# Rewriting the expert stage of a one-core decoder layer: a ring of slots for each of two gathered tables, and the weighted sum shared by TensorE and VectorE

## The reference, cut to what matters

```
a   = gelu(einsum('td,thkd->thk', h, u[e]))        # 128 dot products of 1024 for each token
out = einsum('thk,thkd->td', gate * a, v[e])       # 128 weighted rows summed
x   = x + g2 * out;  y = rms_norm(x, final_g)
```

## Time and profile before

| | us |
|---|---|
| median of 3 runs | 6320.8 |
| span of the profiled execution, first to last instruction | 6308.8 |
| what lies around the span (median less span) | 12.0 |
| expert stage, first instruction to the end of the span (3239.70 to 6308.8) | 3069.1 |
| POOL busy in the whole span | 2370.1 |
| DVE busy in the whole span | 2487.9 |
| PE busy in the whole span | 4576.8 |

### The profile page before, as it was taken

How to read it: one execution, slowest core, us unless ns; L and a number is a source line. 1 busy time by engine, 2 the same in 40 slices (tenths; PEclk the granted TensorE clock), 3 DMA queues, 4 the chain that set the end, 5 groups by cost and what they waited for, 6 DMA issues and landing times. The chain is left out here.

```text
span 6308.8 us, 40559 instructions
## 1 busy us (share of the span) xinstructions
PE 4576.8 (73%) x11996; PEld 2161.0 (34%) x12036; DVE 2487.9 (39%) x5373; ACT 897.6 (14%) x1904; POOL 2370.1 (38%) x2136
## 2 busy tenths in 40 slices
PE   6999999976777767877746657656666566566666
PEld 2444444434444443433212222222222222222222
DVE  2000000004443344799974443443544444444434
ACT  1000000012222210111101011111111111111111
POOL 0000000000000000000037777777777777777776
PEclk8999999987767777988868878878878888788788
DMA  6144434641010033111049999999999999999998
GB/s 238 49 143 142 139 121 142 211 177 50 28 45 37 33 137 147 54 43 39 9 154 338 357 361 366 366 351 368 365 359 369 354 368 366 352 369 356 363 365 302
DMA packets 395337, 1409.24 MB, mean 223 GB/s; under 512 B 39803, under 2 KB 91683, under 8 KB 390500
## 3 DMA queue, kind: packets, MB, share of 16 engines
q0 software_dynamic: 297504, 1083.18, 45.8%
q1 hardware_dynamic: 72118, 272.53, 12.3%
q10 hardware_dynamic: 25664, 52.88, 2.2%
HBM read 1341.66 MB, written 159.08 MB: 238 GB/s over the span
## 5 line engine op out<-in xcount | busy, mean ns | idle before, releaser
L1577 PE MATMUL ex_acc<-ex_V,ex_diag 128*128 128x512 f32 x4096 | 1916.5, 631 | 960.3 <-ACT ex_diag L1601 882.1
L1663 DVE CUSTOM_DVE_ANT_0 ex_U<-ex_U,ex_h 128x1024 f32<-128x1024 f32 x1024 | 1195.5, 1223 | 1560.5 <-DMA ex_U<-in_peer_u,ex_idx 1438.7
L1577 PEld LDWEIGHTS ex_acc<-ex_V,ex_diag 128*128 128x128 f32 x4096 | 827.8, 204 | 2047.1 <-issue 1094.3
L1534 POOL DMA_INDIRECT ex_U<-in_peer_u,ex_idx x1024 | 1178.4, 1151 | 362.3 <-issue 334.8
L1534 POOL DMA_INDIRECT ex_V<-in_peer_v,ex_idx x1024 | 1150.6, 1124 | 312.1 <-issue 308.1
L390 PE MATMUL z_ps<-win,hT 128*128 128x464 f32 x3024 | 1188.0, 554 | 14.6 <-ACT z_stage L372 9.5
L390 PEld LDWEIGHTS z_ps<-win,hT 128*128 128x128 f32 x3024 | 538.9, 179 | 663.0 <-issue 648.5
L1518 POOL DMA_INDIRECT ex_U<-in_peer_u,ex_idxT x8 | 7.6, 949 | 1868.0 <-DVE ex_idxT L1631 1865.9
L466 POOL DMA_DIRECT2D mx_masks<-table_masks x1 | 0.7, 706 | 1362.3 <-POOLq L139 1362.3
L720 DVE TENSOR_SCALAR mx_xb<-mx_O,mx_ab 128x128 f32<-128x128 f32 x32 | 9.0, 344 | 1233.1 <-PE mx_O L533 1233.1
L1596 ACT ACTIVATE ex_u<-ex_u 128x16 f32<-128x16 f32 x64 | 13.8, 216 | 2478.6 <-DVE ex_u L1442 2082.7
(11 more groups left out here) (333 smaller groups left out, 3429.2 us busy)
## 6 DMA issues: line engine op xcount, KB each, us to landing
out_kv_w_sample<-in_cache_kv_w SPq DMA_DIRECT2D x8, 8188.0 KB, 41.6
win<-in_w_in SPq DMA_DIRECT2D x21, 1856.0 KB, 10.1
z_scratch<-z_stage ACTq DMA_DIRECT2D x21, 1856.0 KB
ada<-in_ada_w SPq DMA_DIRECT2D x12, 2048.0 KB, 7.8
ex_U<-in_peer_u,ex_idx POOLq DMA_INDIRECT x1024
ex_V<-in_peer_v,ex_idx POOLq DMA_INDIRECT x1024
out_kv_w_sample<-in_cache_kv_w SPq DMA_DIRECT2D x8, 2044.0 KB, 17.1
mx_zg<-z_scratch SPq DMA_DIRECT2D x8, 1544.0 KB, 7.2
```

What stands on the lines that cost most here:

```text
L1534: pool.indirect_dma_start(out=buf[n][:, :], out_offset=None, in_=table, in_offset=bass.IndirectOffsetOnAxis(ap=idx[b][:, n:n + 1], axis=0) ...
L1577: last = nc.tensor.matmul(acc[:, b, :], dg[:, n, :], V[n][:, b * 512:(b + 1) * 512], start=False, stop=False)
L1663: nc.vector.tensor_tensor_reduce(out=U[n][:, :], in0=U[n][:, :], in1=h2[:, :], scale=1.0, scalar=0.0, op0=ALU.mult, op1=ALU.add, accum_out ...
```

## The change

All slots are numbered through, 0 to 1023 for the prompt and 1024 to 1031 for the samples, and every engine's program is written out slot by slot, without loops.

- U and V have rings of 12 buffers each; slot n uses buffer n % 12. POOL issues 4 gathers of U, then 4 of V, and so on. Each gather waits for the use of the slot 12 earlier. The indices are read where routing left them, without a copy.
- DVE waits for each U slot by itself, makes its dot, and after every 4 slots the gelu for these 4: now through Tanh, in four small operations with the Tanh on ACT between the third and the last.
- The weighted sum is shared. Odd slots go to PE as before, with 4 diagonal buffers. Even slots are summed on DVE: `acc = V * w + acc`, a `scalar_tensor_tensor` on 128 x 1024 with V and acc in SBUF (for the first slot of a tile `tensor_scalar` without acc).
- The tail adds acc to PE's sum first, one operation more. The store moves from ACT's queue to SP's. There are two h2 buffers.
- The samples come last, after the prompt's gathers; their gathers, too, wait for slots of the ring.

```diff
 def experts(k, misc):
+GRP, RING, DIAGS = 4, 12, 4
+def on_pe(slot): return slot >= PROMPT_SLOTS or slot % 2 == 1
...
             @block.gpsimd
-                pool.wait_ge(s["idxT"], 1)
-                for n in range(NS):
-                    pool.indirect_dma_start(out=U[HALF + n][:, :], ...)
-                    pool.indirect_dma_start(out=V[HALF + n][:, :], ...)
-                def head(i, pair, b):
-                    nc.gpsimd.tensor_copy(idx[b][:, :], k.idx[:, bass.ds(i * P + h * NSLOT, NSLOT)])
...
+                def gather_u(slot, index):
+                    if slot >= RING:
+                        pool.wait_ge(s["dots"], slot - RING + 1)
+                    pool.indirect_dma_start(out=half(slot), out_offset=None, in_=u_dram,
+                                            in_offset=bass.IndirectOffsetOnAxis(ap=index, axis=0)).then_inc(loaded[slot % RING], 16)
+                def gather_v(slot, index):
+                    if slot >= RING:
+                        before = slot - RING
+                        if on_pe(before):
+                            pool.wait_ge(s["pe_slots"], pe_upto[before + 1])
+                        else:
+                            pool.wait_ge(s["dve_slots"], dve_upto[before + 1])
+                    pool.indirect_dma_start(out=value(slot), ...).then_inc(v_loaded[slot % RING], 16)
+                for g in range(NG):
+                    for slot in range(g * GRP, g * GRP + GRP):
+                        gather_u(slot, k.idx[:, slot:slot + 1])
+                    for slot in range(g * GRP, g * GRP + GRP):
+                        gather_v(slot, k.idx[:, slot:slot + 1])
+                pool.wait_ge(s["idxT"], 2)
+                for n in range(NS):
+                    gather_u(PROMPT_SLOTS + n, idxT[:, n:n + 1])
+                    gather_v(PROMPT_SLOTS + n, idxT[:, n:n + 1])
...
             @block.tensor
+                    for slot in mine:
+                        pe.wait_ge(v_loaded[slot % RING], 16 * (slot // RING) + 16)
+                        pe.wait_ge(s["diag"], n + 1)
+                        for b in range(2):
+                            last = nc.tensor.matmul(out[:, b, :], diag[:, n % DIAGS, :], value(slot)[:, b * 512:(b + 1) * 512], ...)
...
             @block.vector
+                for g in range(NG):
+                    for slot in range(g * GRP, g * GRP + GRP):
+                        dve.wait_ge(loaded[slot % RING], 16 * (slot // RING) + 16)
+                        nc.vector.tensor_tensor_reduce(out=half(slot), in0=half(slot), in1=h2[i % 2][:, :], ...).then_inc(s["dots"], 1)
+                    if g and g % GT == 0:
+                        tail(i - 1, P, g2[:, :], x1[:, :])
+                    gelu_argument(g, a[:, cols], cube[:, cols], arg[:, cols], ag[:, cols], k.gate[:, g * GRP:g * GRP + GRP])
+                    weight(g, w[:, cols], th[:, cols], ag[:, cols])
+                    for slot in range(g * GRP, g * GRP + GRP):
+                        if on_pe(slot):
+                            continue
+                        at_least(dve, s["dve_slots"], n)
+                        dve.wait_ge(v_loaded[slot % RING], 16 * (slot // RING) + 16)
...
+                            nc.vector.scalar_tensor_tensor(out=acc[:, :], in0=value(slot), scalar=w[:, c:c + 1], in1=acc[:, :],
+                                                           op0=ALU.mult, op1=ALU.add).then_inc(s["dve_slots"], 1)
+                tail(TILES - 1, P, g2[:, :], x1[:, :])
```

More of the change, by code:

```diff
@@ L1433, with on_pe, pe_slots @@
 GELU_C = float(np.sqrt(2.0 / np.pi))
[L1436 to L1442, removed]
+GRP = 4
+RING = 12
+DIAGS = 4
+SLOTS = PH * TOPK
+PROMPT_SLOTS = TILES * SLOTS
+def on_pe(slot):
+    return slot >= PROMPT_SLOTS or slot % 2 == 1
+def pe_slots(slot):
+    return sum(on_pe(n) for n in range(slot))
@@ L1445, in experts, with dve_slots @@
+def dve_slots(slot):
+    return slot - pe_slots(slot)
 def experts(k, misc):
     nc = k.nc
[L1448 to L1458, removed]
+    SL = slice(0, NS)
+    NG = PROMPT_SLOTS // GRP
+    GT = SLOTS // GRP
+    s = {n: k.sem("ex_" + n) for n in (
+        "const", "half_gain", "sample_rows", "h2", "x1", "idxT_ps", "idxT", "nsel", "picked", "dots", "cube", "arg", "gated", "tanh", "weights", "diag",
+        "pe_slots", "dve_slots", "summed", "out", "square", "var", "root", "y", "stored", "masked")}
@@ L1475, in experts @@
+        h2s, x1s = f.sb("ex_h2s", [NS, D]), f.sb("ex_x1s", [NS, D])
+        aS, cubeS, argS, agS, thS, wS = (f.sb("ex_s" + n, [P, NS]) for n in ("a", "cube", "arg", "ag", "th", "w"))
+        out = f.ps("ex_out", [P, 2, 512])
+        row = [f.ps(f"ex_row{b}", [P, 2, 512]) for b in range(2)]
         tp = f.ps("ex_tp", [P, 2 * NS])
@@ L1477, in experts @@
         eye8 = misc[:, C_PICK + NS * NS:C_PICK + 2 * NS * NS].rearrange("p (n m) -> p n m", m=NS)
[L1478 to L1484, removed]
+        outf = out[:, :, :].rearrange("p b n -> p (b n)")
+        half = lambda slot: U[slot % RING][:, :]
+        value = lambda slot: V[slot % RING][:, :]
         with nc.Block() as block:
@@ L1496, in tile @@
[L1496 to L1509, removed]
@@ L1555, in _ @@
-                pe.wait_ge(s["wm"], 1)
+                        last = nc.tensor.matmul(row[n % 2][:, b, :], nsel[:, n, :], h2s[:, b * 512:(b + 1) * 512], start=True, stop=True)
+                    last.then_inc(s["picked"], 1)
+                pe.wait_ge(s["masked"], 1)
+                pe.wait_ge(s["out"], 3 * TILES)
                 for n in range(NS):
-                    pe.wait_ge(vs[n], 16)
-                for b in range(2):
-                    for n in range(NS):
-                        last = nc.tensor.matmul(acc[SL, b, :], wm[:, n, :], V[HALF + n][:, b * 512:(b + 1) * 512], start=(n == 0), stop=(n == NS - 1))
@@ L1611, in tile, with tail @@
[L1611 to L1619 removed]
+                def tail(i, R, src):
+                    act.wait_ge(s["out"], 3 * i + 3)
+                    nc.scalar.activation(junk[0:R, :], src, ACT.Square, accum_out=rs[0:R, 0:1]).then_inc(s["square"], 1)
+                    act.wait_ge(s["var"], 2 * i + 2)
+                    nc.scalar.activation(rs[0:R, 1:2], rs[0:R, 0:1], ACT.Sqrt).then_inc(s["root"], 1)
```

284 lines of the change are left out of this document (125 added, 159 removed).

## The result

The changed kernel takes 6538.5 us (median of 4 runs, 6515.8 to 6541.7) against 6321.4 (6319.5 to 6323.6) of the kernel before, measured beside it: ratio 1.0338, 95% interval 1.0321 to 1.0354. Slower by 3.4%; the forecast was 6565, slower by 3.9%. The profiled execution was the shortest of the four, 6515.8 us, with a span of 6514.0.

What follows compares the result with a forecast made beforehand. POOL's gathers, held by DVE operations with two SBUF operands, were taken as the bound. Stage start 3239.9 + 64 heads 3247 + end 66.5 = 6553, plus 12.0 outside the span: 6565 us, 3.9% slower; range 6310 to 6790.

Steps and rivals of the forecast that it cites:

- The bound: Last stage: everything waits for POOL's gathers, 1.47 us each, lengthened by DVE operations with two SBUF operands.
- The sums hold gathers too: POOL beside DVE: the 8 new sums per head hold gathers like the 16 dots, read from the gather at 3698.16.
- The price, 0.45 for all 24 alike: POOL beside DVE: each of 24 dots and sums per head costs 0.45 us of hold, between 0.376 and 0.52.
- Head and stage: Prompt gathers: 39.9 + 24 x 0.45 = 50.7 us per head of 32, 64 heads 3247 us, starting at 3239.9.
- End: After the last prompt gather: landing, tails, samples' picks 20.8, samples' sums 15.5, store and closing; 66.5 us in all.
- Around the span: Outside the profiled span: 12.0 us between it and the median time, added to the forecast.
- What was costed at nothing: Last stage: slower PE clock covered, POOL not waiting for ring buffers, loading written-out code taken as nothing; 0 us.
- in step: Rival, POOL beside DVE: gathers start as operations end, price near 0.10, 6027 us; chance 0.15 together with "the sums do not hold".
- the sums do not hold: Rival, POOL beside DVE: only dots hold gathers, 16 x 0.376 per head, about 6257 us; within the shared 0.15.
- The transfers: Rival, DMA: transfers are the bound, a gather costs 1.47 us either way, about 6325 us, no change; chance 0.05.
- Locked out: Rival, POOL beside DVE: gathers wait out whole runs of operations, some 7740 us, at half of that 6807; chance 0.08.
- What the gather waits for: POOL's gathers: those of 1.89 and 1.97 us deny that two-operand operations leave descriptor writing unstalled, which would give the floor, 5944.

Runs made afterwards that it cites:

- half rows: Changed kernel with each gathered row cut to 2 KB, other halves of the buffers zero, DVE and PE instructions as before: 6541 us.
- Half the data: Changed kernel with all sums on PE and gathers of 2 KB rows: 6141 us; the same kernel with whole rows took 5989 us.

## Why the prediction was right, point by point

- **The bound.** Right: POOL, through held gathers. The runs with operands in PSUM show it in both kernels, half rows in the changed one.
- **The sums hold gathers too.** Right, from one row of the kernel before: 0.69 us each. That row was misread: the gather at 3698.16 starts 0.23 us before the operation's end, not in its last tenth of a microsecond, and the 0.11 it loses is what the rule above gives for 1.05 us into a sum (1.16 - 1.05).
- **The price, 0.45 for all 24 alike.** Right as a sum (0.434), wrong in its terms. The dots were put up from 0.376 and went down to 0.29; the sums are dearer than the bound of 0.52 that was set from dots. The step that failed is to take one price for each operation and add: the price depends on how the operations are spaced against the gathers. That the terms cancelled was luck. The 1.17 us called a dot's length is the step from one dot to the next (busy time by count, while dots overlap); a dot takes 1.22.
- **Head and stage.** 50.7 us forecast; (6447.13 - 3232.10) / 64 = 50.2 measured. The stage began at 3231.4 instead of 3239.7, a difference between executions that no term held; the first gather followed 0.7 us later.
- **End.** 66.5 against 66.8; picks 20.8, samples' sums 16.1 for 15.5, tail 7.8 for 7.9.
- **Around the span.** 12.0 us was too much: 1.8 in the profiled execution. In all later runs of the kernel before, span and time are 2.1 to 2.6 us apart, so most of the 12.0 came from a profiled execution that was faster than the median. Here both errors of some 8 to 10 us fell within the spread of the runs.
- **What was costed at nothing.** PE's matmul went from 631 to 903 ns at a granted clock of 0.70, 1513.6 / 512 = 2.96 us per slot, covered as argued. POOL waited for PE 10.7 us in all. No cost of the written-out code was found: POOL's idle time stayed at 0.30 us per gather.
- **The rival "in step".** It got 0.15 together with "the sums do not hold" (6257). For the changed kernel both are false. Where the sums are kept from holding, the dots fall into step as well, and the time is 5990 instead of 6257: as separate cases each was priced wrongly.
- **The transfers.** Rejected by half rows. The 358 GB/s that the Trainium skill gives as a core's HBM limit (page "DMA: Bandwidth & Descriptors", section "Where 436 GB/s comes from") is passed for 500 us on end, with one core at work, by the 410 of the kernel before with h2 in PSUM.
- **Locked out.** No gather took over 2.0 us. Why one took 19.54 us before was not tried; with h2 in PSUM none did.
- **What the gather waits for.** The Trainium skill infers that `tensor_tensor` does not stall descriptor writing (page "SBUF — State Buffer", section "Who interferes with whom"). The prediction says that the gathers of 1.89 and 1.97 us deny this; that goes too far. A gather's instruction also reads its column of indices from SBUF, and whether that read or the writing waits was not separated in any run. What the runs show is that the same dots hold a gather with two operands in SBUF and let it pass with one.

## What to carry to other kernels

Where POOL issues the gathers, look at the mean of its gathers before any busy share: if it is above that of an undisturbed one, find the operations of VectorE with two SBUF operands beside them and move one operand to PSUM. Here that is worth 5.4% to the old kernel, with a few lines. Do not carry the price of such a hold from one kernel to another: it depends on how the operations are spaced against the gathers' cycle. Count the holds in the new kernel's own trace, add them to POOL's own pace, and take the transfers' floor if that is higher.

## What was not expected of the hardware

Half the data took longer: 6141 against 5989 us. A gather that is held ends 2.04 us after the dot began, wherever it started, so that the cheapest spacing of the dots is neither the tightest nor the loosest: at 1.23 to 1.32 us gathers pass nearly free, at 1.15 every second dot can cost a hold of about 1.03 us, and at about 1.90 each costs 0.64. And an operation with a single operand, `tensor_scalar` from SBUF to SBUF, holds gathers too: 1.25 to 1.39 us instead of 0.94, at each of the 8 tiles.
